# A mixture-of-experts kernel in fp32: the down product is turned, and one norm moves to VectorE

## The reference

```python
def moe(x, w_router, router_bias, w_gate, w_up, w_down):
    combine = route(t, w_router, router_bias)          # 16 experts, 2 per row
    h = silu(einsum('td,edf->tef', t, w_gate)) * einsum('td,edf->tef', t, w_up)
    y = einsum('tef,efd->td', h * combine[:, :, None], w_down)

for i in range(2):
    ...                                                # mixer i gives mix
    x = layer_norm(ALPHA * x + mix, ln1_g[i], ln1_b[i])
    x = layer_norm(ALPHA * x + moe(x, ...), ln2_g[i], ln2_b[i])
```

## Time and profile before

| | |
|---|---|
| median of 3 runs | 1211.73 us (1211.29 to 1215.57) |
| the profiled execution's own time | 1213.42 us |
| its span | 1211.7 us |
| mean granted TensorE clock | 0.93 |
| expert stage of layer 0, TensorE | 476.34 to 762.26 us |
| first gather to first next-layer expert tile | 769.10 to 884.51 us |
| expert stage of layer 1, TensorE | 884.51 to 1171.12 us |

### The profile page before, as it was taken

The page is one execution under the profiler, slowest core; times in us unless marked ns, Lnnn a source line. Parts: engine busy times, 40 slices in busy tenths (PEclk is TensorE's granted clock), DMA queues, the critical chain, the costliest instruction groups (busy, mean ns, idle before and its releaser), DMA issues.

```text
span 1211.7 us, 28356 instructions
## 1 busy us (share of the span) xinstructions
PE 1054.5 (87%) x11923; PEld 740.8 (61%) x11923; DVE 370.1 (31%) x798; ACT 194.0 (16%) x428; POOL 111.2 (9%) x184
## 2 busy tenths in 40 slices
PE   7899999899899932999999999178189999999985
PEld 6677777544444322677677668067067776776752
DVE  1334444322433251111111111497511111111117
ACT  1234444400222112000000000131020000000000
POOL 0001001030033103000000000321300000000012
PEclk9999999899999965999999999677589999999997
DMA  9324335230023097999999999606359999999915
GB/s 342 146 86 133 106 112 178 82 79 1 1 78 92 26 392 274 350 384 392 395 385 394 397 389 392 215 3 246 141 200 387 386 395 391 387 400 389 377 51 201
DMA packets 80864, 296.04 MB, mean 244 GB/s; under 512 B 10184, under 2 KB 41168, under 8 KB 72495
## 3 DMA queue, kind: packets, MB, share of 16 engines
q1 hardware_dynamic: 53351, 247.50, 54.5%
q10 hardware_dynamic: 19712, 26.75, 6.5%
q0 software_dynamic: 7760, 21.24, 5.1%
HBM read 255.80 MB, written 40.11 MB: 244 GB/s over the span
## 4 chain that ended last, share of the span: by engine, by line
PE 83%; DVE 7%; DMA 4%; POOL 2%; issue 2%; ACT 2%; ACTq 0%; SPq 0%; POOLq 0%; DVEq 0%
PE PS L896 19%; PE PS L874 15%; PE PS L884 14%; PE PS L801 5%; PE PS L573 4%; PE PS L738 4%; PE PS L620 3%; PE PS L636 3%; PE PS L761 2%; PE PS L529 2%; PE PS L629 2%; PE PS L719 2%; PE PS L551 2%; POOL expert_rows L1036 2%; PE PS L806 1%
## 5 line engine op out<-in xcount | busy, mean ns | idle before, releaser
L896 PE MATMUL PS<-ring,arena 128*96 128x512 f32 x512 | 227.4, 597 | 0.0
L874 PE MATMUL PS<-arena,ring 128*64 128x96 f32 x4096 | 180.5, 250 | 53.5 <-DVE arena L1649 53.5
L874 PEld LDWEIGHTS PS<-arena,ring 128*64 128x64 f32 x4096 | 174.4, 140 | 77.4 <-issue 77.4
L884 PE MATMUL PS<-arena,ring 128*64 128x96 f32 x4096 | 174.4, 246 | 0.0
L884 PEld LDWEIGHTS PS<-arena,ring 128*64 128x64 f32 x4096 | 170.9, 137 | 0.0
L896 PEld LDWEIGHTS PS<-ring,arena 128*96 128x96 f32 x512 | 80.8, 163 | 123.0 <-issue 119.2
L1649 DVE STREAM_TRANSPOSE arena<-arena 128x768 uint32<-128x768 uint32 x34 | 54.2, 1593 | 206.7 <-ACT arena L1227 176.6
L1669 DVE COPY arena<-PS 96x512 f32<-96x512 f32 x32 | 22.0, 687 | 218.0 <-PE PS L896 218.0
L1231 ACT ACTIVATE arena<-PS 96x512 f32<-96x512 f32 x32 | 19.0, 593 | 379.3 <-PE PS L896 379.3
L801 PE MATMUL PS<-ring,arena 128*128 128x512 f32 x128 | 55.7, 594 | 0.7 <-issue 0.7
L1002 POOL DMA_DIRECT2D ring<-cache_krope x64 | 34.6, 541 | 141.3 <-issue 141.3
(11 more groups left out here) (245 smaller groups left out, 1061.2 us busy)
## 6 DMA issues: line engine op xcount, KB each, us to landing
ring<-w_gate SPq DMA_DIRECT2D x32, 2048.0 KB, 15.2
ring<-w_up SPq DMA_DIRECT2D x32, 2048.0 KB, 15.9
ring<-w_down SPq DMA_DIRECT2D x32, 2048.0 KB, 16.3
arena<-expert_rows ACTq DMA_DIRECT2D x144, 96.0 KB, 9.6
expert_out<-arena ACTq DMA_DIRECT2D x32, 384.0 KB, 8.3
expert_rows<-ring SPq DMA_DIRECT2D x6, 1920.0 KB, 10.1
ring<-cache_ckv SPq DMA_DIRECT2D x64, 128.0 KB, 2.1
ring<-w_o SPq DMA_DIRECT2D x1, 4096.0 KB, 19.3
```

Source lines behind the costliest of these rows:

```text
L874: last = nc.tensor.matmul(bank(s, KF, CAP)[at:at + 64, f, :], wg[w][:, k, P * f + at:P * f + at + 64], xeT[s][:, k, :], start=(k == 0), st ...
L884: last = nc.tensor.matmul(out[at:at + 64, :], wu[w][:, k, P * f + at:P * f + at + 64], xeT[s][:, k, :], start=(k == 0), stop=(k == KD - 1))
L896: last = nc.tensor.matmul(bank(4 + hf)[0:CAP, :], h[s][:, f, :], wd[w][:, f, 512 * hf:512 * (hf + 1)], start=(f == 0), stop=(f == KF - 1))
```

## The change

1. **Down product.** The weights become the stationary operand, in dense blocks of 64 columns, and `h` moves; the result lies turned in banks 4 and 5 (features on partitions). ScalarE and VectorE copy it to a new buffer `yT`. TensorE turns it back with eight transposes (`turn_back`) behind the first block of the next tile's gate product, into the same banks; then both engines copy the rows to `ys` and ScalarE stores them. `down_ps` counts twice a tile. After the loop one more `turn_back` and copy stand alone. The first tile of a layer turns what lies in `yT` and no one copies it.
2. **Second norm of layer 0.** It takes the form of the first norm, with mean and gains, then deviation and offsets, both on VectorE (`norm`). `normalise`, `spread`, `gain` and `shift` are no longer called; ScalarE keeps the square root. On GpSimd the fifth gather no longer stands behind an add. VectorE finishes a row tile's norm before it takes up the next.

```diff
+        yT = view(arena, 7168, KD, CAP)
...
+                def turn_back(tl):
+                    pe.wait_ge(q["yT_set"], 2 * tl + 2)
+                    for m in range(KD):
+                        last = nc.tensor.transpose(bank(4 + m // 4, 4, P)[0:CAP, m % 4, :], yT[:, m, :], ident)
+                    last.then_inc(q["back_ps"], 1)
...
                     for f in range(KF):
+                        if f == 1:
+                            turn_back(tl)
...
-                    for blocks in (range(KF - 1), (KF - 1,)):
-                        if KF - 1 in blocks:
-                            pe.wait_ge(q["h_set"], 2 * tl + 2)
-                        for hf in range(2):
-                            for f in blocks:
-                                last = nc.tensor.matmul(bank(4 + hf)[0:CAP, :], h[s][:, f, :], wd[w][:, f, 512 * hf:512 * (hf + 1)],
+                    def down(m, blocks):
+                        for f in blocks:
+                            for at in (0, 64):
+                                last = nc.tensor.matmul(bank(4 + m // 4, 4, CAP)[at:at + 64, m % 4, :],
+                                                        wd[w][:, f, P * m + at:P * m + at + 64], h[s][:, f, :],
                                                         start=(f == 0), stop=(f == KF - 1))
-                    last.then_inc(q["down_ps"][s], 1)
+                        return last
+                    down(0, range(KF - 1))
+                    down(4, range(KF - 1))
+                    pe.wait_ge(q["h_set"], 2 * tl + 2)
+                    down(0, (KF - 1,))
+                    down(4, (KF - 1,))
+                    for m in (1, 2, 3, 5, 6, 7):
+                        last = down(m, range(KF))
+                        if m in (3, 7):
+                            last.then_inc(q["down_ps"][s], 1)
...
+                turn_back(2 * nh)
...
+                def store(tl, s, count):
+                    act.wait_ge(q["back_ps"], tl + 2)
+                    act.wait_ge(q["y_st"][s], count)
                     nc.scalar.activation(ys[s][0:CAP, 0:512], bank(4)[0:CAP, :], ACT.Copy).then_inc(q["y_set"], 1)
                     act.wait_ge(q["y_set"], 2 * tl + 4)
                     act.dma_start(yd[bass.ds(CAP * tl, CAP), :], ys[s][0:CAP, :]).then_inc(q["y_st"][s], 16)
+                def tile(u, s, more):
+                    tl = 2 * u + s
+                    act.wait_ge(q["xeT_set"], tl + 1)
+                    load_rows(s, bass.ds(CAP * (tl + 2), CAP))
+                    if more:
+                        store(tl - 1, 1 - s, 16 * (u + s))
+                    act.wait_ge(q["gate_ps"][s], u + 1)
+                    nc.scalar.activation(sg[s], bank(s, KF, CAP), ACT.Silu).then_inc(q["sg_set"], 1)
+                    act.wait_ge(q["down_ps"][s], 2 * u + 1)
+                    nc.scalar.activation(yT[:, 0:4, :], bank(4, 4, CAP), ACT.Copy).then_inc(q["yT_set"], 1)
...
+                def rows_back(tl, s, count):
+                    dve.wait_ge(q["back_ps"], tl + 2)
+                    dve.wait_ge(q["y_st"][s], count)
+                    v.tensor_copy(ys[s][0:CAP, 512:D], bank(5)[0:CAP, :]).then_inc(q["y_set"], 1)
...
+                    dve.wait_ge(q["down_ps"][s], 2 * u + 2)
+                    v.tensor_copy(yT[:, 4:8, :], bank(5, 4, CAP)).then_inc(q["yT_set"], 1)
...
-                for i in range(NT):
+                if L == 0:
+                    gather(4)
+                for i in range(NT if L else 0):
                     shift(L, i)
...
-                    normalise(0, step)
+                    deviation(0, 1, step)
...
-                    stats(0, 1, step)
-                if 2 <= step <= NT:
-                    gain(0, step - 1)
-                if step < NT:
-                    spread(0, step)
-                if step == 0:
-                    gain(0, 0)
+                    norm(0, 1, step)
```

More of the change, by code:

```diff
@@ L338, in expert_sems @@
             two = ("wg_ld", "wu_ld", "wd_ld", "xe_ld", "y_st", "gate_ps", "up_ps", "down_ps")
-            one = ("xeT_set", "sg_set", "h_set", "y_set")
+            one = ("xeT_set", "sg_set", "h_set", "yT_set", "back_ps", "y_set")
             return {n: [sem(f"{n}{s}_{L}") for s in range(2)] for n in two} | {n: sem(f"{n}_{L}") for n in one}
@@ L1211, in experts @@
                 act.sem_inc(q["y_set"], 1)
+                for s in range(2):
+                    act.sem_inc(q["y_st"][s], 16)
                 act.wait_ge(scat, 160 * (L + 1))
@@ L1239, in experts @@
                     tile(u, 1, True)
+                store(2 * nh - 1, 1, 16 * nh)
             def take_pages(b):
@@ L1503, in stats, with norm @@
                 v.bn_aggr(mv[0:n, i, :], bn[0:n, i, :]).then_inc(ln_agg, 1)
-            def norm1(L, i):
-                n = rows_of(i)
-                x, gains, offsets = X[0:n, i, :], gb[0:n, 0, :], gb[0:n, 1, :]
-                stats(L, 0, i)
+            def norm(L, which, i):
+                n, k = rows_of(i), NT * which + i + 1
+                x, gains, offsets = X[0:n, i, :], gb[0:n, 2 * which, :], gb[0:n, 2 * which + 1, :]
+                stats(L, which, i)
                 if i == 0:
-                    dve.wait_ge(gb_ld[L][0], 32)
-                dve.wait_ge(ln_agg, 2 * NT * L + i + 1)
+                    dve.wait_ge(gb_ld[L][which], 32)
+                dve.wait_ge(ln_agg, 2 * NT * L + k)
                 link(v.scalar_tensor_tensor(out=x, in0=x, scalar=mv[0:n, i, 0:1], in1=gains, op0=ALU.subtract, op1=ALU.mult))
-                dve.wait_ge(ln_std, 2 * NT * L + i + 1)
+                dve.wait_ge(ln_std, 2 * NT * L + k)
                 link(v.reciprocal(rstd[0:n, i:i + 1], std[0:n, i:i + 1]))
@@ L1654, in experts, with tile @@
                 turn_rows(0)
-                def tile(u, s, stored):
+                def rows_back(tl, s, count):
+                    dve.wait_ge(q["back_ps"], tl + 2)
+                    dve.wait_ge(q["y_st"][s], count)
+                    v.tensor_copy(ys[s][0:CAP, 512:D], bank(5)[0:CAP, :]).then_inc(q["y_set"], 1)
+                def tile(u, s, more):
                     tl = 2 * u + s
+                    if more:
+                        rows_back(tl - 1, 1 - s, 16 * (u + s))
                     dve.wait_ge(q["sg_set"], tl + 1)
@@ L1665, in tile @@
                     v.tensor_tensor(h[s][:, KF - 1, :], sg[s][:, KF - 1, :], bank(6 + s, CAP), ALU.mult).then_inc(q["h_set"], 1)
[L1666 to L1669 removed]
+                    dve.wait_ge(q["down_ps"][s], 2 * u + 2)
+                    v.tensor_copy(yT[:, 4:8, :], bank(5, 4, CAP)).then_inc(q["yT_set"], 1)
                 tile(0, 0, False)
[L1672 removed]
+                tile(0, 1, True)
                 with dve.Fori(1, nh) as u:
@@ L1679, in _ @@
             for i in range(4):
-                norm1(0, i)
+                norm(0, 0, i)
             samples()
-            norm1(0, 4)
+            norm(0, 0, 4)
             route(0)
@@ L1705, in _ @@
                         dve.wait_ge(pool_out, 32)
-                    norm1(1, step - 4)
+                    norm(1, 0, step - 4)
             route(1)
```

33 lines of the change are left out of this document (13 added, 20 removed).

## The result

| | before | after |
|---|---|---|
| median | 1213.47 us (4 runs) | 1199.19 us (4 runs, 1196.43 to 1202.33) |
| ratio | | 0.9883, 95% interval 0.9849 to 0.9917 |
| the profiled execution, its span | 1213.42, 1211.7 us | 1200.12, 1197.9 us |

The kernel became 1.2% faster: 14.3 us by the medians, 13.8 us by the spans of the two profiled executions. 17.2 were forecast for the execution, and the time forecast, 1195 us, lies 4 us under the measured median.

What follows compares the result with a forecast made beforehand. TensorE bounds at 17.75 us a tile, the weight stream close at 17.95. Gains of 5.0 + 3.8 + 8.4 = 17.2 us from 1213.4 give 1196.2, 1194.5 as median, forecast 1195; own range 1191 to 1200, 8 in 10 1190 to 1205.

Steps and rivals of the forecast that it cites:

- rival (b): Expert loops: weight stream slows or shifts 3 us beyond the slack, loops gain 7 to 8 each, 1199 us; chance 0.15.
- The stages: Expert stages of both layers: 16 tiles 10.2 us less per layer, at most about 12.7 less 1.1 by the weight stream.
- idle TensorE before the down product of the last three tiles: Expert loop, sign of being wrong: TensorE idle before a product of the last tiles means the weight stream decides.
- The down product and the turn: Expert tile: three products of 5.28 us plus 1.27 for transposes and geometry changes, 17.11 us, 0.64 less.
- (a): Expert tile: the turned block is dear, a tile of 17.5 us, kernel 1204 us; chance 0.16.
- (c): Expert tile: the turn saves nothing, a tile of 17.7 us, kernel 1210 us, no change; chance 0.08.
- (d): Expert tile: TensorE waits for late evictions before the transposes, kernel slower, about 1233 us; chance 0.05.
- (e): Expert tile: the turned block drops TensorE's clock to 1.2 GHz, a tile of 19.05, kernel 1250 us; chance 0.02.
- still lands near 744.3: End of layer 0's loop: last down matrix lands there plus at most 1.1 us, leaving 1.4 to 2.5 us of slack.
- Behind the stage of layer 0: First layer's last store: issued at 754.8, 8.4 us to landing, lands at 763.2 for 768.2, 5.0 us gained.
- The norms: Between the stages: VectorE no sooner at the next layer's norms, last full mix earlier, 3.8 us gained.
- The last turn: After a layer's last tile: nothing covers the turn, 1.8 us more before the store; second layer gains 8.4.

Runs made afterwards that it cites:

- next_late: Changed kernel with the next layer's first expert load held back until layer 0's third row-tile sum: ratio 0.9834; control, same edit on the kernel before: 0.9982.
- step2: Changed kernel with w_down loaded in two runs of 8 KB a partition instead of four of 4 KB, gate and up columns at step 2: ratio 0.9879.
- two_turned: Changed kernel with two of the eight transposes in each turn, full weights: ratio 0.9834 to the kernel before.

## Why the prediction was right, and where it was off

The measured time lies in the forecast's own range, and the tile came out as worked out, for the reasons given. But the measured 1199 us is also the figure of rival (b), which had a chance of 0.15, and so are its parts: 4 us at the first store, 6 in the second layer and 3.8 between, for 4.2, 5.9 and 3.6 measured. Only half of its reason came, as said under *The stages*. One of the signs of being wrong was there as well, idle TensorE before the down product of the last three tiles.

*The down product and the turn.* 5.28 us as forecast; 1.16 us for turn and changes of geometry for 1.27. The tile is 17.00 us, 0.11 better than the sum. The evictions were covered as said. Rivals (a), (c) and (d) fall with the tile's length. So does (e): the clock was granted at 1.00, 2.4 GHz, through all three windows above, and from 911 to 1156 us in layer 1, with a block of transposes in each tile. The Trainium skill (TensorE: Matmul & The Clock Gate, "Part 4: PE-mode transpose") would have let one fear for it; eight transposes between products of 16 us did not bring the clock down here.

*The stages.* 16 tiles at 17.00 would have given 12.0 us a layer; the sum said 10.2; measured 8.3 and 7.2. This is the term that was mis-sized: 4.9 us over both layers, of which other terms gave back 1.5, to the 3.4 by which the sum was off. Two things took it, about half each. One is the stream, rival (b)'s mechanism: the last three tiles of layer 0 were 17.45, 17.86 and 17.92 us (2.2 us over), those of layer 1 17.56, 17.91 and 17.74 (2.2). The last down matrix landed at 748.2, 3.9 us later than before, where I had allowed at most 1.1: the sentence that it "still lands near 744.3" took the stream's 17.95 us a tile as fixed. It depends on where the rows fall in it. That is 1.4 us past the 746.8 at which the sum wanted it, where rival (b) spoke of 3 us beyond the slack. Time to landing was 30.1 us in the last tile, not about 26. The Trainium skill (DMA: Bandwidth & Descriptors, "Where 436 GB/s comes from") has a ceiling of 435 GB/s, and says that for transfers between memory and SBUF about 358 GB/s binds. The prediction took up the first figure alone; the full engines moved 378 to 394 here, between the two, and the floor was real. The kernels with half matrices and with two transposes show the stream to be the cause. The other was in no step of the prediction and in no rival: the second tile of layer 0 lasted 18.58 us and that of layer 1 19.25, 1.6 and 2.25 us over, with TensorE idle on "issue". The packets of instructions described above point to the fetch of the longer loop body; an experiment on it is missing. That stream and stops together came to rival (b)'s figure is luck.

*Behind the stage of layer 0.* The store landed at 763.26; forecast 763.2. That came of two errors that cancel, issue 1.8 us later and landing 6.70 instead of 8.4 us. `next_late` and its control show the mechanism: the next layer's weights were in the way.

*The norms.* The order was right: VectorE came no sooner to the next layer's norms (34.6 us before, 34.6 after), and the gain was the last mix, 3.0 us instead of 3.8. VectorE's wait for it did not go, as the signs had it, but fell from 3.71 to 1.92 us. The small pooling matmuls took 6.6 us for 5.2, since the clock fell to 1.2 GHz in the midst of them, after a stretch in which TensorE had been busy at 2.4 (a pair of records took 0.38 us, then 0.59), so the mix ended 53.1 us after the first sum and not by 52.1. The window (us, busy us of PE, PEld, DVE, ACT and POOL, clock, DMA share, GB/s):

```profile
815.00:819.00 4.00, 4.00 (x16) 3.74 (x17) 3.90 (x5) 0.48 (x2) 0.00 (x0) 0.50 0.99 419
```

That VectorE is freed of GpSimd's blocks (three of 1.96 us) made no difference, as the one full-width operation that each of the five row tiles has more (1.28 us) costs about the same.

*The last turn.* 1.8 us from product to store more than before, as forecast; 0.5 us of it came back further on, which I have not taken apart.

*Slips in the working.* The down product before was eight matmuls, seen as sixteen records, not sixteen matmuls. Rival (d) adds up to 1236.5 us (1235 on the median's scale) and not 1233, and rival (e) to 1255 (1251 with the norms' gain) and not 1250. Rival (b)'s 1199 lacks the 1.7 us between the profiled execution and the median that the others have; with them it is 1198. None of this changes the forecast.

## What to carry to other kernels

When two resources are full, take the slower one's time between landings and ask for how many tiles the buffer still hides it: a saving on the faster one is paid out only until then, and an unchanged transfer that comes behind the stage is met sooner. An operand that is turned to fill the array can be worth its transposes, if independent products of at least the evictions' length stand ahead of them (0.66 us of exposure per tile took back all of the gain here). After such a change look at what was prefetched "because the buffer was free"; held back until needed, it gave 5 us. And look at more than the matrices: in `step2` these were on time and the rows were late.

## What was not expected of the hardware

- Stationary columns with a step of 4 words in SBUF took 217 ns to load (64 columns, fp32) where steps of 1 and 2 took 137 and 138.
- The DMA engines at a constant share of 1.02 moved between 378 and 394 GB/s, by the phase between the row loads (1 KB packets) and the weights (16 KB for gate and up, 4 KB for down); with runs of 8 KB for down (`step2`) the landing intervals were even, and the rows took up to 31 us to land.
- The first pass of a loop with 784 TensorE records for 544 had stops of 0.2 to 0.9 us (up to 2.1 in `two_turned`) to which the profile gives no releaser; all 35 of them end 1.2 to 1.6 us after a 16 KB packet of instructions.
